# mLSTM scan of the prompt over convolved inputs, and four orders of the first stage

## The reference

```python
u_c = silu(causal_conv(u_m)).reshape(bsz, seq, 4, 256)           # 4 heads, DK = 256
q = einsum('blhd,hde->blhe', u_c, w_mq)
k = einsum('blhd,hde->blhe', u_c, w_mk) * 256 ** -0.5
v = v_m.reshape(bsz, seq, 4, 256)
# chunks of 128 tokens; carry (c, n, m), zero at the start for the prompt
att = einsum('bthd,bshd->btsh', qc, kc) * exp(dmat - m_t[:, :, None])
num = einsum('btsh,bshv->bthv', att, vc) + w_inter[..., None] * einsum('bthd,bhdv->bthv', qc, c)
den = att.sum(axis=2) + w_inter * einsum('bthd,bhd->bth', qc, n)
c_new = w_old[..., None, None] * c + einsum('bsh,bshd,bshv->bhdv', w_s, kc, vc)
n_new = w_old[..., None] * n + einsum('bsh,bshd->bhd', w_s, kc)
```

## Time and profile before

| | us |
|---|---|
| median of 3 timed executions | 3401.12 |
| the profiled execution, whole | 3379.47 |
| its span | 3377.6 |
| PE busy | 3095.7 (92%) |
| DVE busy | 2540.3 (75%) |
| POOL busy | 1719.3 (51%) |
| ACT busy | 936.9 (28%) |
| mean granted clock of PE | 0.967 of full speed |

### The profile page before, as it was taken

One profiled execution on the slowest core, in us unless ns is written; L12 is line 12 of the kernel. 1 busy time (PEld: TensorE's weight loads), 2 busy tenths in 40 slices (PEclk: granted clock), 3 DMA queues, 4 the chain that ended last, 5 costly groups with the idle time before them and its releaser, 6 DMA issues.

```text
span 3377.6 us, 42522 instructions
## 1 busy us (share of the span) xinstructions
PE 3095.7 (92%) x13799; PEld 2051.9 (61%) x13799; DVE 2540.3 (75%) x5369; ACT 936.9 (28%) x2145; POOL 1719.3 (51%) x1419
## 2 busy tenths in 40 slices
PE   9999999999878898988877659999999999999998
PEld 8997887887333233333244436777677766777765
DVE  7771053888578898999889967778777767777777
ACT  3122212665111122112278761111111111111112
POOL 3332131443136676777745546555555555555554
PEclk9999999999989999999998789999999999999999
DMA  4435466677659999999989999999999999999997
GB/s 152 103 78 174 158 218 217 231 269 289 235 184 360 373 374 368 373 378 377 354 310 356 344 350 386 395 382 394 396 406 393 376 380 372 389 403 389 390 377 272
DMA packets 388783, 1074.51 MB, mean 318 GB/s; under 512 B 58824, under 2 KB 148744, under 8 KB 382176
## 3 DMA queue, kind: packets, MB, share of 16 engines
q0 software_dynamic: 186624, 679.56, 53.0%
q1 hardware_dynamic: 151280, 311.91, 25.9%
q10 hardware_dynamic: 50672, 80.51, 6.5%
HBM read 978.59 MB, written 93.11 MB: 317 GB/s over the span
## 4 chain that ended last, share of the span: by engine, by line
PE 43%; DMA 10%; DVE 10%; issue 7%; POOL 3%; ACT 1%; DVEq 0%; POOLq 0%; SPq 0%; ACTq 0%; PEldq 0%
PE PB L2346 18%; PE PB L2333 14%; DMA vbf<-in_peer_v,gixv 5%; PE PB L2322 3%; PE PB L2373 3%; PE PB L2309 3%; DMA x1d<-in_peer_u 3%; DVE ub L1994 3%; POOL vbf L1722 2%; DMA ub<-in_peer_u,gix 2%; POOL ub L1722 1%; DVE ohb L1941 1%; PE PB L2417 1%; DVE oha L1939 1%; PE PB L2291 1%
## 5 line engine op out<-in xcount | busy, mean ns | idle before, releaser
L1722 POOL DMA_INDIRECT ub<-in_peer_u,gix x640 | 701.1, 1095 | 707.0 <-DVE hid L1994 500.5
L2346 PE MATMUL PB<-vbd,wd 128*128 128x512 f32 x1536 | 685.3, 596 | 0.0
L2333 PE MATMUL PB<-xds,uts 128*128 128x384 f32 x3072 | 568.9, 339 | 0.0
L2333 PEld LDWEIGHTS PB<-xds,uts 128*128 128x128 f32 x3072 | 531.2, 189 | 0.5 <-issue 0.5
L1722 POOL DMA_INDIRECT vbf<-in_peer_v,gix x340 | 396.0, 1165 | 159.1 <-issue 99.2
L2346 PEld LDWEIGHTS PB<-vbd,wd 128*128 128x128 f32 x1536 | 283.8, 191 | 309.9 <-issue 309.9
L2373 PE MATMUL PB<-vbf,dg 128*64 128x512 f32 x1200 | 319.8, 656 | 97.4 <-DMA vbf<-in_peer_v,gixv 92.5
L1722 POOL DMA_INDIRECT vbf<-in_peer_v,gixv x300 | 325.1, 1084 | 163.7 <-issue 92.5
L1955 DVE TENSOR_TENSOR uts<-PB,uts 128x512 fp32r<-128x512 f32 x256 | 175.8, 687 | 301.3 <-ACT uts L2168 301.1
L1994 DVE CUSTOM_DVE_ANT_0 ub<-ub,x1g 128x1024 f32<-128x1024 f32 x257 | 313.2, 1222 | 51.2 <-DMA ub<-in_peer_u,gix 41.3
L2168 ACT CAST uts<-PB 128x512 fp32r<-128x512 f32 x256 | 150.1, 586 | 644.8 <-PE PB L2322 632.0
(11 more groups left out here) (427 smaller groups left out, 5097.7 us busy)
## 6 DMA issues: line engine op xcount, KB each, us to landing
vbd<-in_peer_v SPq DMA_DIRECT2D x128, 512.0 KB, 7.0
x1d<-in_peer_u SPq DMA_DIRECT2D x96, 512.0 KB, 9.1
gd_d<-stag ACTq DMA_DIRECT2D x12, 2048.0 KB, 9.9
gbd<-gd_d SPq DMA_DIRECT2D x16, 1536.0 KB, 18.4
ubd<-in_peer_u SPq DMA_DIRECT2D x32, 512.0 KB, 9.5
wtr<-in_w_tok SPq DMA_DIRECT2D x6, 2048.0 KB
tok_d<-stg ACTq DMA_DIRECT2D x48, 256.0 KB, 2.0
rb_e<-rows_d SPq DMA_DIRECT2D x8, 1536.0 KB, 10.8
```

Source lines behind the costliest of these rows:

```text
L1722: pool.indirect_dma_start(out=buf, out_offset=None, in_=a[table], in_offset=bass.IndirectOffsetOnAxis(ap=index, axis=0)).then_inc(done, 16)
L2333: last = T.matmul(PB[:, 6, 0:TD], uts[:, b % 2, ul, k, :], xds[:, xl, k, :], start=(k, n) == (0, 0), stop=(k, n) == (KD - 1, 2))
L2346: last = T.matmul(PB[:, 2 * d + n, :], wd[:, b % 2, d * CH:(d + 1) * CH], vbd[b % 8][:, n * 512:(n + 1) * 512], start=b == 0, stop=b == NB ...
```

## The change

1. **Order of the PEER products.** `pick_tiles` puts the products of the first tile behind units 4, 6, 7, 8 in place of 2, 4, 6, 8.
2. **Low half of the row weights.** DVE makes `wtkl`, ahead of its loop over `xl`; POOL made it.
3. **Row stores.** ACT's 14 DMAs of gate rows go out after three channel pairs, no longer after the channel loop.
4. **Sample units.** ACT's function over `ssum` and its store come two units later (t == 1), behind two prompt units.
5. **The mLSTM state of the prompt.** With u the convolved input, q = u Wq and k = u Wk / 16, the scores q k' are u (Wq Wk' / 16) u'. The 4 matrices M = Wq Wk' / 16 (`mu0`, `mu1`) are made once: 32 transposes and 4 `weight_product`, copied by ACT and DVE, in tiles that are free then (`mix`, `mixT`). In a chunk q~ = u M takes the place of q; u takes the place of k in transposes, scores and the state, so `cst` holds the sum over u. The projection to k and ACT's copy of it are gone. At the scan's end `cst` goes to DRAM whole (`cu_d`).
6. **The state is turned at the end.** Behind the last PEER sums SP loads `w_mk` and `cu_d` (2.07 MB), PE multiplies them (16 matmuls of 256 columns and 16 of one), ACT scales, copies and stores `p_c` and `p_n` among the stores of y.

```diff
+def pick_tiles(j):
+
+    return () if j >= NHC // 4 else (2, 4, 6, 8) if j else (4, 6, 7, 8)
...
-                            if u % 9 in (2, 4, 6, 8) and 2 * i + q < NHC // 4:
-                                w_product(2 * i + q, u % 9 // 2 - 1)
+                            if u % 9 in pick_tiles(2 * i + q):
+                                w_product(2 * i + q, pick_tiles(2 * i + q).index(u % 9))
...
-                    chan_out(0, 0)
-                    for i in steps(act, NCT // 2 - 1):
+                    def chan_pair(i):
                         chan_out(i, 1)
                         chan_silu(i, 0)
                         chan_out(i + 1, 0)
                         chan_silu(i, 1)
-                    chan_out(NCT // 2 - 1, 1)
-                    for q in range(2):
-                        chan_silu(NCT // 2 - 1, q)
+
+                    chan_out(0, 0)
+                    for i in range(3):
+                        chan_pair(i)
                     act.wait_ge(s_rr, 1)
                     for src, r, n in ((nacs, R_NACS, NH), (mrun, R_M, MH), (wlog, R_WLOG, MH),
                                       (dtr, R_DT, NH), (ir, R_G, MH), (mt, R_MT, MH)):
@@ -466,6 +472,12 @@
                         act.dma_start(rows_s_d[r:r + n, :], src[0:n, SEQ:NTOK]).then_inc(s_rs, 16)
                     act.dma_start(o["p_m"], mcar[:, NCH:NCH + 1]).then_inc(s_rs, 16)
                     act.dma_start(o["s_m"], mt[:, SEQ:NTOK]).then_inc(s_rs, 16)
+                    for i in steps(act, NCT // 2 - 1, 3):
+                        chan_pair(i)
+                    chan_out(NCT // 2 - 1, 1)
+                    for q in range(2):
+                        chan_silu(NCT // 2 - 1, q)
+
...
+                            if t == 1:
                                 act.wait_ge(s_su[q], i + 1)
-                                nc.scalar.activation(stg[b][0:NSMP, :], ssum[:, :], func).then_inc(s_sf[q], 1)
+                                nc.scalar.activation(stg[9 * q % 6][0:NSMP, :], ssum[:, :], func).then_inc(s_sf[q], 1)
                                 act.wait_ge(s_sf[q], i + 1)
-                                tok_out(i, u, NSMP, b)
+                                tok_out(i, 9 * q, NSMP, 9 * q % 6)
...
-                            if u % 9 in (2, 4, 6, 8) and 2 * i + q < NHC // 4:
-                                w_store(2 * i + q, u % 9 // 2 - 1)
+                            if u % 9 in pick_tiles(2 * i + q):
+                                w_store(2 * i + q, pick_tiles(2 * i + q).index(u % 9))
...
                     pool.wait_ge(s_wr, 16)
-                    split(wrp, wrow, s_rh, s_rp, 1)
+                    pool.sem_inc(s_go, 1)
+                    nc.gpsimd.tensor_copy(wrp[0][:, :, :], wrow).then_inc(s_rh, 1)
...
+                    dve.wait_ge(s_rh, 1)
+                    nc.vector.tensor_tensor(wrp[1][:, :, :], wrow, wrp[0][:, :, :].bitcast(f32), ALU.subtract).then_inc(s_rp, 1)
...
+            def weight_product(h):
+                pe.wait_ge(s["wk_kept"], h + 1)
+                pe.wait_ge(s["wq_kept"], h + 1)
+                for d in range(KT):
+                    for e in range(KT):
+                        last = T.matmul(PB[:, 4 + h, d * DK:(d + 1) * DK], wqT[:, h, e, d * P:(d + 1) * P], wkT[:, h, e, :],
+                                        start=e == 0, stop=e == KT - 1)
+                last.then_inc(s["m_made"], 1)
+
+            pe.wait_ge(s_pre, 80)
+            for h in range(MH):
+                for w, bank in ((wmk, 4 + h), (wmq, h)):
+                    for k in range(KT):
+                        for e in range(KT):
+                            last = T.transpose(PB[:, bank, e * DK + k * P:e * DK + (k + 1) * P], w[:, h, k, e * P:(e + 1) * P], ident[:, :])
+                    last.then_inc(s["w_turned"], 1)
+            weight_product(0)
+            weight_product(1)
+            pe.wait_ge(s["wq_kept"], MH)
...
                 free(pe, s["dve_c2"], i)
                 if i == 0:
-                    pe.wait_ge(s["setup"], 1)
-                    pe.wait_ge(s["wqk"], 32)
-                for w, b, done in ((wmk, 6, "pe_bk"), (wmq, 4, "pe_b")):
-                    for h in range(MH):
-                        for e in range(KT):
-                            for k in range(KT):
-                                last = T.matmul(two(b)[:, (h * KT + e) * CH:(h * KT + e + 1) * CH],
-                                                w[:, h, k, e * P:(e + 1) * P], cht[:, UT0 + h * KT + k, :],
-                                                start=k == 0, stop=k == KT - 1)
-                    last.then_inc(s[done], 1)
-                pe.wait_ge(s["act_k"], i + 1)
+                    weight_product(2)
+                    weight_product(3)
+                for h in range(MH):
+                    if i == 0:
+                        pe.wait_ge(s["m_kept"], h + 1)
+                    for e in range(KT):
+                        for k in range(KT):
+                            last = T.matmul(two(4)[:, (h * KT + e) * CH:(h * KT + e + 1) * CH],
+                                            mu(h)[:, k, e * P:(e + 1) * P], cht[:, UT0 + h * KT + k, :],
+                                            start=k == 0, stop=k == KT - 1)
+                last.then_inc(s["pe_b"], 1)
+                pe.wait_ge(s["act_xt"], i + 1)
                 pe.sem_inc(s["passed"], 1)
                 for j in range(MH * KT):
-                    last = T.transpose(two(0)[:, j * P:(j + 1) * P], kT[:, j, :], ident[:, :])
+                    last = T.transpose(two(0)[:, j * P:(j + 1) * P], cht[:, UT0 + j, :], ident[:, :])
                 last.then_inc(s["pe_kk"], 1)
                 pe.wait_ge(s["act_qk"], i + 1)
                 for h in range(MH):
                     for k in range(KT):
-                        last = T.matmul(PB[:, 2, h * CH:(h + 1) * CH], kT[:, h * KT + k, :], qT[:, h * KT + k, :],
+                        last = T.matmul(PB[:, 2, h * CH:(h + 1) * CH], cht[:, UT0 + h * KT + k, :], qT[:, h * KT + k, :],
                                         start=k == 0, stop=k == KT - 1)
                 last.then_inc(s["pe_st"], 1)
                 if i == 0:
...
                 for h in range(NH):
                     if h == 2:
-                        act.wait_ge(s["pe_bk"], i + 1)
-                        free(act, s["pe_st"], i)
-                        S.activation(kT[:, :, :].rearrange("p a n -> p (a n)"), two(6), ACT.Copy, scale=DK ** -0.5).then_inc(s["act_k"], 1)
-                    if h == 10:
                         act.wait_ge(s["pe_b"], i + 1)
                         free(act, s["pe_nx"], i)
                         S.copy(qT[:, :, :].rearrange("p a n -> p (a n)"), two(4)).then_inc(s["act_qk"], 1)
...
             act.wait_ge(s["dve_c2"], NCH)
-            S.copy(nst[:, :].unsqueeze(2), cst[:, :, DK:DK + 1]).then_inc(ss["nst"], 1)
-            act.dma_start(o["p_c"], cst[:, :, 0:DK]).then_inc(s["outs"], 16)
-            act.wait_ge(ss["nst"], 1)
-            act.dma_start(o["p_n"], nst[:, :]).then_inc(s["outs"], 16)
+            act.dma_start(cu_d, cst[:, :, :]).then_inc(s["outs"], 16)
...
+            def keep_turned(h):
+                dve.wait_ge(s["w_turned"], 2 * h + 1)
+                V.tensor_copy(wkT[:, h, :, :].rearrange("p e d -> p (e d)"), PB[:, 4 + h, :]).then_inc(s["wk_kept"], 1)
+
+            def keep_product(h):
+                dve.wait_ge(s["m_made"], h + 1)
+                V.tensor_scalar(mu(h).rearrange("p k e -> p (k e)"), PB[:, 4 + h, :], DK ** -0.5, None, ALU.mult).then_inc(s["m_kept"], 1)
+
             V.memset(onec[:, :], 1.0)
-            V.memset(hT[:, :], 0.0)
-            V.memset(cst[:, :, :], 0.0)
+            for tile in (numr, orow, grow, emr):
+                V.memset(tile[:, :], 0.0)
+            keep_turned(0)
+            keep_turned(1)
+            V.memset(cst[:, :, :], 0.0).then_inc(ss["zeroed"], 1)
+            keep_turned(2)
+            keep_turned(3)
+            V.memset(qsm[:, :], 0.0)
+            keep_product(0)
             V.memset(qkr[:, :, :], 0.0)
             V.memset(onesq[:, :], 1.0)
-            for tile in (qsm, numr, orow, grow):
-                V.memset(tile[:, :], 0.0)
-            V.memset(emr[:, :], 0.0).then_inc(ss["zeroed"], 1)
+            keep_product(1)
+            V.memset(hT[:, :], 0.0)
             V.memset(v1[:, :, DK:DK + 1], 1.0).then_inc(s["setup"], 1)
-            dve.wait_ge(s["setup"], 1)
             cp = Chain(dve, c_p, 0, s["passed"])
...
                 V.tensor_tensor(heads(xdt[:, :], HD), heads(xtok[:, :], HD), wide(cols[q][:, R_DT:R_DT + NH], HD), ALU.mult).then_inc(s["dve_xdt"], 1)
+                if i == 0:
+                    keep_product(2)
+                    keep_product(3)
...
+                sp.wait_ge(s["ws"], NBLK)
+                sp.dma_start(wk, a["w_mk"]).then_inc(s["cul"], 16)
+                sp.dma_start(cu, cu_d).then_inc(s["cul"], 16)
...
-                for d in range(-1, ND):
```

(29 more changed lines are left out.)

41 lines of the change are left out of this document (26 added, 15 removed).

## The result

The kernel after takes 3414.97 us (median of 6 timed executions, 3410.57 to 3420.65), the kernel before 3400.35 beside it: a ratio of 1.0048, 95% interval 1.0025 to 1.0070. It is slower by 8.5 to 24 us; the median lies inside the predicted range and 5 us above the predicted time.

What follows compares the result with a forecast made beforehand. It took PE as the bound in the first stage, and PE and DVE as one loop in the scan's chunks. The terms summed to +8.4 on the profiled 3379.47: 3388, or 3410 at the median's distance; range 3390 to 3428.

Steps and rivals of the forecast that it cites:

- First stage: PE's 7.35 us wait for ACT's copy of the first PEER product goes, and the slow product behind it: -8.8 us.
- The loop of PE and DVE: In chunks 1 to 7, of the 3.57 us leaving PE only 0.63 comes off the loop: -4.4 us.
- PE alone as the bound: Rival for the scan: PE was the sole bound, so 7 x 3.57 = 25 us come off: 3376; chance 0.09.
- The clock: Ahead of the SSD outputs, PE's new wait of 2.9 to 3.0 us lowers its clock in chunks 1 to 7: +11.6 us.
- the price of one fall: A fall of PE's clock behind a wait costs 1.66 us, taken from eight equal matmuls in PEER: 1.94 against 3.60.
- The forecast's upper end: Scan clock term: twice 1.66 us each time if the low clock lasts over a further stretch, +23.2 us.
- the slower rival: Low clock holds over the SSD outputs and the stretch behind them in each chunk: 3421, or 3427 with the loads; chance 0.10.
- the row of 3.02: PEER profile row: eight matmuls took 3.60 us behind a 3.02 us wait; the new scan wait was priced by it.
- First chunk: Set-up of the new matrices makes the first SSD outputs start at 595.7, not 588.84: +7 us, between 5 and 9.
- The further fall there: First chunk: PE waits twice about 2.5 us; one more clock fall would be +1.7 us, put at +1.
- End of the program: Turning the state behind the last PEER sums moves the end by 0.5 to 4 us, taken as +2.
- the loads: SP's 2.07 MB at the end could displace the last gathers, up to +5.6 us; taken as none.

Runs made afterwards that it cites:

- e2: Kernel after with the mix-row transposes ahead of the scores in chunks 1 to 7; 3406.88 us, ratio 1.0007.
- e5: Kernel after with half of the turn (16 of its 32 matmuls) put ahead of the last gathered sum; 3389.39 us.
- e1: Kernel after with eight unread matmuls filling PE's wait ahead of the SSD outputs in chunks 1 to 7; 3403.3 us, ratio 1.0001.
- e6: Kernel after without the turn at the end, state stored raw at the scan's end, SP's two late loads kept but unread; 3404.54 us.
- e7: Kernel after without the four orders of the first stage; 3412.26 us.
- e8: Kernel after without the four first-stage orders, with the mix-row transposes ahead of the scores; 3385.74 us.

## Why the prediction was right, step by step

- **First stage.** -8.8 forecast, -9.44 measured, of which 9.0 behind the start of the channel tiles. PE's wait and the slow product went as said. The low half of the row weights was costed at nothing. The channel tiles start at 20.87 and not 21.32; over all kernels they start at 20.84 to 21.80 with it and 21.32 to 22.43 without, 0.7 us apart on average, so it gave some tenths. That each of two orders alone would do was not foreseen. Two readings were off without harm to the sum. Of the 3.69 us for `ssum` 2.17 stayed. And most of the 8.33 us ahead of ACT's first unit was not waiting for the stores to land but ACT issuing the 14 of them, 263.63 to 269.83 before:

```profile
263.63 1.15 ACTq L465 DMA_DIRECT2D rows_d<-t  x1
...
269.51 0.32 ACTq L468 DMA_DIRECT2D out_s_m<-t  x1
```

- **The loop of PE and DVE.** Right: 3.57 us left PE and 0.91 came off the chunk (30.70), forecast 0.63. PE alone as the bound would have given 28 us, and is out.
- **The clock.** The mechanism was right; the step that failed is the price of one fall, 1.66 us from the earlier trace rows, where a chunk lost 3.3. In the earlier trace rows 1.66 us was the whole loss: the group behind the slow one ran at its usual pace, and the granted clock from 1171.75 to 1178 was 1.00 again.

```profile
1171.67 3.70 PE L2309 MATMUL PB<-wp_first,x1T 128*128 128x512 f32 x8
```

In the scan the low clock lasted about twice as long and went on behind the outputs into `hT` times `cht` (0.61 over 8.80 us). So the price of a fall in one place of the program did not hold for another; why it lasts longer here is open. The forecast's upper end, twice 1.66, is what happened; it was the slower rival's mechanism. "Nearest to the row of 3.02" was no ground either: 2.60 in e2 and the 2.56 in three chunks of e5 did nothing, while 2.56 elsewhere did. That a fall came in every chunk of the kernel after is in part luck: of e5's chunks 1 to 6 three had none.
- **First chunk.** +7 forecast, +6.39 measured. The further fall there, +1, didn't come in the profile of after; it did in e1, e6, e7 and e8, for 3.3 to 3.4 each.
- **End of the program.** +2 forecast, +6.21 measured. The turn was right (2.1); the loads, taken at none because some 13 us lay between, cost 4.0, within the bound of 5.6. The Trainium skill's rule that I set beside it ("DMA: Bandwidth & Descriptors", section "Issuing engines are not separate DMA queues": DMAs of all issuing engines interleave on the same 16 DMA engines) was the better guide, and e6 agrees with 4.97 us of waiting.
- **Sum.** The terms -8.8 - 4.4 + 11.6 + 7 + 1 + 2 gave +8.4; measured they are -9.4 - 6.4 + 23.1 + 6.4 + 0 + 6.2, and -1.3 at PEER's start: +18.6. The median moved by +14.6. The two misses, 11.5 us of the clock and 4.2 of the end, both went the slower way and were each inside their stated ends. That the forecast stands only 5 us off is partly luck: the other terms and the wait at PEER's start came out 5.5 us lower together, and the median moved 4 us less than the profiles' sum.

## What to carry to other kernels

When work leaves an engine that looks full, follow the engine it waits for through one whole round: here 0.9 of 3.6 us came off, because the other half of the loop was as long. A PE that is then left waiting a few us per round can lose more to its clock (3.3 us here) than the removal gains (0.9), so reorder until its waits stand where slack follows, or leave them filled. And a one-off step placed at the very end competes with the transfers that end there; the cheap part of a change (here the orders of the first stage, -0.5%) is worth measuring without the rest.
